# Three buffers freed in the output-weight stage, and expert weights laid out eight rows a partition

## The chip, the cores and the metric

The kernel runs on one NeuronCore of a Trainium2 chip. The metric is the device time of one execution in microseconds (us). Three runs of the kernel before took 727.13, 729.30 and 731.64 us; the median is 729.3. Lower is better.

## The reference, cut to what matters

Two transformer blocks over 256 tokens of width 1024, all float32. The first block has one layer: a hybrid mixer (three kinds of attention) and a hierarchical mixture of 32 experts. The second has two layers of attention.

```
y = hybrid_mixer(x, w_in, w_out, ...)            # heads A, B, C joined, then @ w_out (1024 x 1024)
x = layer_norm(ALPHA * x + y, ln1_g, ln1_b)
grp = argmax(x @ w_route_group + b)              # router: one of 4 groups,
top_val, top_idx = top_k(x @ w_route_expert, 2)  # then 2 of its 8 experts
y_e = (silu(x_e @ w_gate[e]) * (x_e @ w_up[e])) @ w_down[e]   # w_gate, w_up: 1024 x 256, w_down: 256 x 1024
x = layer_norm(ALPHA * x + sum of gate * y_e, ln2_g, ln2_b)
x = second_block(x, mem_2, ...)                  # two layers
```

The kernel reads the weights of all 32 experts, 1 MiB for each of gate, up and down (96 MiB).

## The kernel before, in words

**Engines.** The program is one instruction stream per engine. SP issues nearly all weight loads, in one fixed order; each may first wait on a semaphore, and every later load stands behind it. PE multiplies, ACT and DVE copy, normalise and split, POOL issues small loads and the vectors of the layer norms.

**Memory.** `ring` holds 12 slots of 1 MiB (8 KB in each of 128 partitions). Before the expert stage the same bytes have other names (the `with nc.sbuf_tensor` block): slots 0 to 4 receive raw weights, slots 5 to 7 are `w_high`, 8 to 10 `w_low`, 11 `a_high`. `x_low` shares its bytes with `xT`, `mix_low` with `mixT`. Nine more buffers of 1 MiB outside the ring also receive expert weights: halves of `bias`, `probsT`, `mixT`, `xT`, `k_c`, two parts of `tiles`, and the top of `values` (`beyond_ring`).

**Three products for one.** Before the experts, float32 accuracy comes from three products: weights and inputs are split into a high part (ACT, `high`, L1664) and a low part (DVE, `low`, L2336); `product` (L909 to L911) multiplies high by high, high by low and low by high. `SPLITS` lists the splits, `SPLIT_AT` the job at which each is made. `w_high` and `w_low` go round in six half-slot units. The jobs `tile1` and `bv` are input products; `y1` (s, tt) is one 256-column block s of the output product for token half tt. Their order is `Y_ORDER`, then come `x1t` (x turned), `logit` (router) and `rank`.

**Between y1 and the experts.** DVE takes each y1 into `x2` (L1959), forms mean and variance, then `centred` (L2110, two halves of 512) and `scaled` or `scaled_half` (L2118, L2124). The router works on x as it is ahead of the norm: PE turns it, ACT writes it to `xT` (L1504), PE multiplies (L1073). `choose`, `rank` and `locate_first` give every token its place in the experts' rows.

**The expert stage.** Experts are handled in 8 bunches of 4. Each bunch has 12 loads of 1 MiB: item j = 0 to 3 the first half of the 1024 input rows of gate and up for its four experts, j = 4 to 7 the second half, j = 8 to 11 the down weights. Below, expert load n is item n % 12 of bunch n // 12. PE's order in bunch b: `gate_up` half 0 and half 1 (L1324, 32 matmuls each), `gather` of bunch b + 1 (L1280: x is the stationary operand, 128 x 128 pieces), `turn_hidden` (L1299), `down` (L1339), `add_back` (L1307, into PSUM banks 0 to 3). In bunch 0, after gate_up half 1, four `diagonal` products put ALPHA * x in these banks (L1413). Between add_back of bunch 6 and gate_up of bunch 7 stands a test of a flag (`more_rounds`). In bunch 7 PE runs filling matmuls (L1271) ahead of down.

**Who frees a buffer.** `expert_slots` (L143 to L156) deals out buffers: loads 0 to 20 take those of `FIRST_LOADS`; four of them (`ONCE`) are used once; the other 17 go round in the order of the load's number. So load 21 takes load 0's buffer, and so on to load 83. For the last bunch the first four loads must take slots 0, 1, 2, 3 (`NEXT_LAYERS`), since the next layers' weights follow there. `free_for_experts` (L738) holds SP until the last user of that buffer is done, by `expert_done`: j < 4 after half 0 of gate_up, j < 8 after half 1 (`gu_ready`), j >= 8 after down (`y_ready`).

**The order of SP's work around the change** (`for n in range(FIRST_EXPERT)`, then `FIRST_LOADS`): w_out0, w_out1, w_out2 and w_out3 into slots 0, 1, 2, 0, w_out3 once w_out0 is split; load 2 into `k_c`; loads 16, 17, 18 once the last B scores are read; 3, 4 (`probsT`, top of `values`) once the attention is done; 5, 6, 7 into slots 1, 2, 0 once their weights are split; 8 to 15 as the y1 products release the split units; 19, 20. For bunches below `IN_ORDER` = 2 a partition holds rows p, p + 128, ... of gate and up (pieces of 1 KB); from bunch 2 on it holds eight adjacent rows (four to a half: 4 KB), and the gather takes x with a step of eight elements to match.

## Time and profile before

| | |
|---|---|
| median of 3 runs | 729.3 us |
| the profiled execution | 730.15 us |
| its span, first to last instruction | 728.2 us |
| mean granted TensorE clock | 0.969 |
| PE busy | 661.3 us (91%) |
| DVE, ACT busy | 353.1 us (48%), 330.1 us (45%) |
| moved by DMA | 167.84 MB, mean 230 GB/s |
| chain of waits by engine | PE 58%, SP's queue 13%, DMA 9%, DVE 8%, ACT 8%, issue 3% |

The page's busy shares are means over stages with different limits. It also cuts the span in 40 slices of 18.2 us; in its DMA line each digit is the busy share of the 16 DMA engines in tenths, and the line under it gives what they moved. Expert loads run from slice 4 on, the expert stage on PE from slice 10 to 22.

### The profile page before, as it was taken

To read this page: it belongs to the slowest core of one execution; us is meant where nothing else is said; L and a number is where in the kernel's file an instruction comes from. 1 tells how busy PE (TensorE), PEld (TensorE's weight loads), DVE (VectorE), ACT (ScalarE), POOL (GpSimd) and SP (SyncE) were. 2 spreads that over 40 slices of the span, in tenths; PEclk is the share of its full clock that TensorE was granted. 3 is DMA by queue.
4 is the path that set the end of the run, shared out by engine and by line. 5 is a ranking of instruction groups with operands and counts; after the bars stand their busy time and mean duration, and the time that the engine had idled before them with its cause. 6 is when DMAs were issued, how large, how long until landed. Compare 5 with 4: busy or idle time off the path is not lost.

```text
span 728.2 us, 11783 instructions
## 1 busy us (share of the span) xinstructions
PE 661.3 (91%) x4605; PEld 513.0 (70%) x4606; DVE 353.1 (48%) x817; ACT 330.1 (45%) x776; POOL 43.8 (6%) x57
## 2 busy tenths in 40 slices
PE   6989999999899999789796999898979999889986
PEld 5967998789545436335262589877859899778876
DVE  1543656645531021011010557787765487877733
ACT  3465656541011122011120354778864647788642
POOL 6001000000000000000000322000000020100000
PEclk9999999999999999898898999999979999999999
DMA  9995327097999999999999857045533080171301
GB/s 275 338 298 173 118 86 232 23 333 280 363 410 412 412 415 409 415 411 411 416 391 409 268 167 237 1 129 162 161 130 116 15 276 1 57 234 60 114 1 59
DMA packets 94682, 167.84 MB, mean 230 GB/s; under 512 B 4271, under 2 KB 75713, under 8 KB 90529
## 3 DMA queue, kind: packets, MB, share of 16 engines
q1 hardware_dynamic: 92272, 160.88, 61.5%
q0 software_dynamic: 2224, 6.10, 2.5%
q8 instruction: 39, 0.64, 0.4%
q14 instruction: 19, 0.15, 0.1%
q10 hardware_dynamic: 128, 0.08, 0.0%
HBM read 165.96 MB, written 1.07 MB: 229 GB/s over the span
## 4 chain that ended last, share of the span: by engine, by line
PE 58%; SPq 13%; DMA 9%; DVE 8%; ACT 8%; issue 3%; DVEq 0%; ACTq 0%
SPq L777 11%; PE psum L909 11%; PE psum L911 10%; PE psum L910 10%; PE psum L1324 4%; PE psum L1280 3%; DMA values<-in_w_expert_down_dram 3%; PE psum L1214 2%; DMA ring<-in_w_expert_up_dram 2%; PE psum L1339 2%; PE psum L952 2%; PE psum L1044 2%; PE psum L1261 2%; SPq L780 2%; DMA ring<-in_w_in_dram 2%
## 5 line engine op out<-in xcount | busy, mean ns | idle before, releaser
L909 PE MATMUL psum<-a_high,w_high 128*128 128x256 f32 x512 | 150.1, 293 | 8.7 <-DVE w_low L2336 4.6
L911 PE MATMUL psum<-a_high,w_low 128*128 128x256 f32 x512 | 145.4, 284 | 0.0
L910 PE MATMUL psum<-x_low,w_high 128*128 128x256 f32 x512 | 145.3, 284 | 0.0
L2336 DVE TENSOR_TENSOR w_low<-ring,w_high 128x1024 fp32r<-128x1024 f32 (+1 forms) x76 | 107.7, 1429 | 17.4 <-ACT w_high L1664 17.4
L909 PEld LDWEIGHTS psum<-a_high,w_high 128*128 128x128 f32 x512 | 98.6, 193 | 18.5 <-issue 6.8
L1664 ACT ACTIVATE w_high<-ring 128x1024 fp32r<-128x1024 f32 (+1 forms) x79 | 96.1, 1220 | 14.1 <-DMA ring<-in_w_in_dram 10.8
L910 PEld LDWEIGHTS psum<-x_low,w_high 128*128 128x128 f32 x512 | 98.7, 193 | 0.1
L911 PEld LDWEIGHTS psum<-a_high,w_low 128*128 128x128 f32 x512 | 98.6, 193 | 0.0
L1324 PE MATMUL psum<-ring,q_c 128*32 128x512 f32 x336 | 64.6, 708 | 13.5 <-DMA ring<-in_w_expert_up_dram 8.0
L909 PE MATMUL psum<-w_high,a_high 128*128 128x256 f32 x240 | 69.9, 291 | 0.1
L910 PE MATMUL psum<-w_low,a_high 128*128 128x256 f32 x240 | 68.7, 286 | 0.0
L1280 PEld LDWEIGHTS psum<-tiles,x_nat 128*128 128x128 f32 x256 | 53.6, 299 | 7.5 <-issue 7.5
L2258 DVE TENSOR_TENSOR tiles<-tiles,psum 128x256 f32<-128x256 f32 x8 | 3.4, 421 | 110.3 <-ACT tiles L1714 110.2
L1280 PE MATMUL psum<-tiles,x_nat 128*128 128x128 f32 x256 | 55.1, 373 | 0.5 <-DVE tiles L2231 0.5
L911 PE MATMUL psum<-w_high,mix_low 128*128 128x256 f32 x192 | 55.0, 286 | 0.0
L909 PEld LDWEIGHTS psum<-w_high,a_high 128*128 128x128 f32 x240 | 46.9, 195 | 3.6 <-issue 2.3
L1712 ACT ACTIVATE tiles<-psum 128x256 f32<-128x256 f32 x8 | 3.1, 384 | 99.9 <-PE psum L1324 99.9
L1324 PEld LDWEIGHTS psum<-ring,q_c 128*32 128x32 f32 x336 | 16.2, 127 | 44.0 <-issue 44.0
L910 PEld LDWEIGHTS psum<-w_low,a_high 128*128 128x128 f32 x240 | 47.0, 196 | 0.0
L911 PEld LDWEIGHTS psum<-w_high,mix_low 128*128 128x128 f32 x192 | 37.7, 197 | 0.0
L1214 PE MATMUL psum<-const,probs 128*128 128x128 f32 x200 | 32.6, 285 | 4.1 <-ACT probsT L1634 3.0
L1634 ACT ACTIVATE probsT<-psum 128x512 f32<-128x512 f32 (+1 forms) x56 | 30.3, 547 | 9.5 <-PE psum L1214 8.6
(343 smaller groups left out, 1148.1 us busy)
## 6 DMA issues: line engine op xcount, KB each, us to landing
ring<-in_w_in_dram SPq DMA_DIRECT2D x36, 1024.0 KB, 9.1
ring<-in_w_expert_down_dram SPq DMA_DIRECT2D x22, 1024.0 KB, 17.7
ring<-in_w_expert_gate_dram SPq DMA_DIRECT2D x42, 512.0 KB, 14.8
ring<-in_w_expert_up_dram SPq DMA_DIRECT2D x42, 512.0 KB, 15.3
ring<-in_w_out_dram SPq DMA_DIRECT2D x12, 1024.0 KB, 5.0
ring<-in_w_mem_kv_dram SPq DMA_DIRECT2D x4, 1024.0 KB, 12.2
k_c<-in_w_expert_down_dram SPq DMA_DIRECT2D x3, 1024.0 KB, 17.4
probsT<-in_w_expert_gate_dram SPq DMA_DIRECT2D x4, 512.0 KB, 15.0
```

The source lines that it names most:

```text
L777: sp.dma_start(to[:, SLOT // 2 * m:SLOT // 2 * m + SLOT // 2].rearrange("p (k n) -> p k n", n=DE), w[:, 4 * half:4 * half + 4, :]).then_in ...
L780: sp.dma_start(to, ins["w_expert_down"][0, e].rearrange("(p k) n -> p (k n)", p=P)).then_inc(loaded[slot_of(n)], 16)
L909: pe.matmul(dst, left[0], right[0], start=first, stop=False)
L910: pe.matmul(dst, left[0], right[1], start=False, stop=False)
L911: return pe.matmul(dst, left[1], right[0], start=False, stop=last)
L952: mm = pe.matmul(dst, src[:, k, P * tt:P * tt + P], w[:, k, a:b], start=(k == 0), stop=(k == KC - 1))
L1214: mm = pe.transpose(dst[:, P * c:P * c + P], pr[:, a:a + P], ident)
L1280: mm = pe.matmul(dst[:, P * c:P * c + P], x[:, k, :], places2[:, tt, :], start=(tt == 0), stop=(tt == 1))
L1324: mm = pe.matmul(bank(6)[PLACES * e:PLACES * e + PLACES, :], gathered2[b % 2][:, k, PLACES * e:PLACES * e + PLACES], w, start=(k == 0), st ...
L1634: act.activation(probsT[:, 512 * (n % 4):512 * (n % 4) + w], bank(t_at(n))[:, 0:w], ACT.Copy).then_inc(turned_out, 1)
L1664: act.activation(split_like_raw(n)[0], raw_of(n), ACT.Copy).then_inc(highs, 1)
L2336: dve.tensor_tensor(w_l, raw_of(n), as_f32(w_h), ALU.subtract).then_inc(lows, 1)
```

## The change

Six edits:

1. The low part of an output weight (`y1`) is written over its raw slot (`slots_low`, the same bytes as slots 0 to 4) and not into `w_low`. The slot is then free when the product has read it, not when it is split. w_out3 goes to slot 8 (`LAST_OUT_SLOT`) in place of slot 0.
2. The router's turned x goes to `q_c` (`x1T`), not to `xT`.
3. Slots 9 and 10 and `xT` take loads 4, 5 and 3 once the last input product (`LAST_INPUT`) is done. SP issues loads 2 and 3, then w_out3.
4. `FIRST_LOADS` has another order, and other buffers for loads 3 to 15 and 20.
5. `IN_ORDER` goes: gate and up weights lie eight rows a partition in all bunches.
6. The first norm writes x in the matching order: `centred` writes to `tiles`, `scaled_half` reads that and writes x with a step of 128 elements (`spread`). The gather then reads adjacent elements in all bunches; the diagonal products read with the step. Tokens 0 to 127 are scaled in two halves, not in one instruction.

```diff
@@ -130,15 +130,14 @@
 EARLY = ((0, 3), (1, 4))
-FIRST_LOADS = EARLY + ((2, K_C), (16, TILES_MID), (17, BIAS_HIGH), (18, BIAS_LOW), (3, PROBS_T), (4, V_TOP), (5, 1),
-                       (6, 2), (7, 0), (8, 6), (9, 9), (10, 7), (11, 10), (12, 5), (13, 8), (14, 11), (15, MIX_T),
-                       (19, LN_ROWS), (20, X_T))
+FIRST_LOADS = EARLY + ((2, K_C), (3, X_T), (4, 9), (5, 10), (16, TILES_MID), (17, BIAS_HIGH), (18, BIAS_LOW),
+                       (6, PROBS_T), (7, V_TOP), (8, 0), (9, 1), (10, 6), (11, 2), (12, 7), (13, 5), (14, 8), (15, 11),
+                       (20, MIX_T), (19, LN_ROWS))
 ONCE = (TILES_MID, BIAS_HIGH, BIAS_LOW, LN_ROWS)
...
 PER_BUNCH = 12
-IN_ORDER = 2
@@ -160,11 +159,14 @@
 TWICE_ROUND, LATE_RING = 2 * MIXERS_RING, 3
+LAST_OUT, LAST_OUT_SLOT = ITEM["w_out3"], 8
 MEM_AT = 3
...
 def slot_of(n):
+    if n == LAST_OUT:
+        return LAST_OUT_SLOT
     if n < FIRST_EXPERT:
@@ -386,7 +388,8 @@
-LAST_SPLIT = {item_split(n): n for n in range(len(SPLITS))}
+LAST_INPUT = max(n for n, _job in enumerate(JOBS) if _job[0] in ("tile1", "bv"))
+LAST_SPLIT = {item_split(n): n for n in range(len(SPLITS)) if SPLITS[n][0] != "y1"}
 OPENING = [SPLIT[("tile1", 0)]] + [SPLIT[("tile2", l, 0)] for l in range(LAYERS)]
@@ -436,7 +439,7 @@
-        with nc.sbuf_tensor("slots_before", [P, MIXERS_RING * SLOT], F32), \
+        with nc.sbuf_tensor("slots_low", [P, MIXERS_RING * SLOT], F32R) as slots_low, \
                 nc.sbuf_tensor("w_high", [P, UNITS * SLOT // 2], F32R) as w_high, \
@@ -469,6 +472,14 @@
+        def spread(row, half):
+
+            return row.rearrange("p (k q) -> p q k", k=KC)[:, P // 2 * half:P // 2 * half + P // 2, :]
+
+        def folded_in(row, half):
+
+            return row[:, 512 * half:512 * half + 512].rearrange("p (q k) -> p q k", k=KC)
+
         def c_(name):
@@ -477,7 +488,9 @@
         x4 = x_nat[:, :].rearrange("p (t k q) -> p t k q", t=2, k=KC)
+        centred2 = tiles[:, 0:2048].rearrange("p (t d) -> p t d", t=2)
         xT3 = xT[:, :].rearrange("p (k t) -> p k t", k=KC)
+        x1T = q_c[:, :].rearrange("p (k t) -> p k t", k=KC)
         y_nat = tiles[:, 0:2048].rearrange("p (t d) -> p t d", t=2)
@@ -487,7 +500,11 @@
             a = units_before(n) % UNITS * KC * P
-            return [w[:, a:a + KC * wide].rearrange("p (k n) -> p k n", k=KC) for w in (w_high, w_low)]
+            high, low = w_high[:, a:a + KC * wide], w_low[:, a:a + KC * wide]
+            if SPLITS[n][0] == "y1":
+                k = slot_of(item_split(n))
+                low = w_low[:, 0:SLOT] if k == LAST_OUT_SLOT else slots_low[:, SLOT * k:SLOT * k + SLOT]
+            return [w.rearrange("p (k n) -> p k n", k=KC) for w in (high, low)]
@@ -744,10 +761,12 @@
                     sp.wait_ge(*expert_done(earlier[-1]))
-                elif k < MIXERS_RING:
+                elif k < MIXERS_RING or k == LAST_OUT_SLOT:
                     used_up(max(m for m in range(FIRST_EXPERT) if slot_of(m) == k))
-                elif k < RING - 1:
-                    owners = {UNIT_OWNER[u] for u in range(units_before(OPENING[1])) if u % UNITS // 2 == (k - 5) % 3}
+                elif k in (9, 10, X_T):
+                    sp.wait_ge(p_ready, LAST_INPUT + 1)
+                elif k < 8:
+                    owners = {UNIT_OWNER[u] for u in range(units_before(OPENING[1])) if u % UNITS // 2 == k - 5}
                     sp.wait_ge(p_ready, max(max(users(n)) for n in owners) + 1)
@@ -759,8 +778,6 @@
                     sp.wait_ge(ln_done, 2)
-                elif k == X_T:
-                    sp.wait_ge(p_ready, JOB[("logit", 1)] + 1)
                 else:
@@ -773,7 +790,7 @@
                     for m, name in enumerate(("w_expert_gate", "w_expert_up")):
-                        w = ins[name][0, e].rearrange("(k p) n -> p k n" if b < IN_ORDER else "(p k) n -> p k n", p=P)
+                        w = ins[name][0, e].rearrange("(p k) n -> p k n", p=P)
                         sp.dma_start(to[:, SLOT // 2 * m:SLOT // 2 * m + SLOT // 2].rearrange("p (k n) -> p k n", n=DE),
@@ -783,7 +800,11 @@
             for n in range(FIRST_EXPERT):
-                if n >= MIXERS_RING:
+                if n == LAST_OUT:
+                    for i in range(2, 4):
+                        load_expert(FIRST_EXPERT + i)
+                    sp.wait_ge(p_ready, LAST_INPUT + 1)
+                elif n >= MIXERS_RING:
                     used_up(max(m for m in range(n) if slot_of(m) == slot_of(n)))
@@ -799,7 +820,7 @@
                     sp.dma_start(bias3[:, 0:A_HEADS, :], shifted_rows(0, A_HEADS)).then_inc(bias_in, 16)
-            for n in [i for i, _ in FIRST_LOADS[len(EARLY):]] + list(range(len(FIRST_LOADS), PER_BUNCH * (BUNCHES - 1))):
+            for n in [i for i, _ in FIRST_LOADS[len(EARLY) + 2:]] + list(range(len(FIRST_LOADS), PER_BUNCH * (BUNCHES - 1))):
                 load_expert(FIRST_EXPERT + n)
@@ -1070,7 +1091,7 @@
                             from_act(("x1t", tt, k // 4))
-                        mm = pe.matmul(dst[:, 0:GROUPS + EXPERTS], xT3[:, k, P * tt:P * tt + P], router[:, k, :],
+                        mm = pe.matmul(dst[:, 0:GROUPS + EXPERTS], x1T[:, k, P * tt:P * tt + P], router[:, k, :],
                                        start=(k == 0), stop=(k == KC - 1))
@@ -1276,8 +1297,7 @@
                     for tt in range(2):
-                        x = x4[:, tt] if b < IN_ORDER else x2[:, tt, :].rearrange("p (q k) -> p k q", k=KC)
-                        mm = pe.matmul(dst[:, P * c:P * c + P], x[:, k, :], places2[:, tt, :],
+                        mm = pe.matmul(dst[:, P * c:P * c + P], x4[:, tt, k, :], places2[:, tt, :],
                                        start=(tt == 0), stop=(tt == 1))
@@ -1411,7 +1431,7 @@
                             pe.matmul(bank(m), diagonal[:, P * (m // 2):P * (m // 2) + P],
-                                      x2[:, m // 2, 512 * (m % 2):512 * (m % 2) + 512],
+                                      spread(x2[:, m // 2, :], m % 2),
                                       start=True, stop=False, skip_group_check=True)
@@ -1501,7 +1521,7 @@
                     tt, half = job[1:]
-                    op = act.activation(xT3[:, 4 * half:4 * half + 4, P * tt:P * tt + P],
+                    op = act.activation(x1T[:, 4 * half:4 * half + 4, P * tt:P * tt + P],
                                         src.rearrange("p (c t) -> p c t", c=4), ACT.Copy)
@@ -2107,7 +2127,8 @@
                 for half in range(2):
-                    op = dve.scalar_tensor_tensor(x_half(tt, half), values(tt, half), mv3[:, tt, 0:1],
+                    to = x_half(tt, half) if n else centred2[:, tt, 512 * half:512 * half + 512]
+                    op = dve.scalar_tensor_tensor(to, values(tt, half), mv3[:, tt, 0:1],
                                                   ln_row[:, 0, 512 * half:512 * half + 512], ALU.subtract, ALU.mult)
@@ -2120,9 +2141,9 @@
-                xs = x_half(tt, half)
-                return dve.scalar_tensor_tensor(xs, xs, ln_rs[:, tt:tt + 1],
-                                                ln_row[:, 1, 512 * half:512 * half + 512], ALU.mult, ALU.add)
+                return dve.scalar_tensor_tensor(spread(x2[:, tt, :], half), folded_in(centred2[:, tt, :], half),
+                                                ln_rs[:, tt:tt + 1], folded_in(ln_row[:, 1, :], half),
+                                                ALU.mult, ALU.add)
@@ -2455,8 +2476,10 @@
                         centred(0, tt, ln1_in, x_half)
+                        dve.wait_ge(ln_rstd, tt + 1)
                         if tt == 0:
-                            scaled(0, 0)
+                            scaled_half(0, 0)
+                            scaled_half(0, 1).then_inc(ln_done, 1)
                         logit_shift(tt)
...
                             scaled_half(1, 0)
```

`spread(row, half)` is row viewed as 64 groups of 8 elements that lie 128 apart; `folded_in` views 512 adjacent elements as 64 groups of 8.

## Rows read from the trace of the kernel before

**Rows 1.** Chain that ended last, 343 to 404 us: start, us, what.

```profile
343.11 15.92 DMA ring<-in_w_expert_up_dram
...
359.17 6.62 PE psum L1324 x32
...
365.80 0.33 SPq L777
...
380.36 21.86 DMA values<-in_w_expert_down_dram
...
402.35 1.88 PE psum L1339 x13
```

**Rows 2.** The page's DMA share and rate in 40 slices.

```profile
DMA  9995327097999999999999857045533080171301
GB/s 275 338 298 173 118 86 232 23 333 280 363 410 412 412 415 409 415 411 411 416 391 409 268 167 237 1 129 162 161 130 116 15 276 1 57 234 60 114 1 59
```

**Rows 3.** Windows: bounds, length, busy per engine, clock, DMA share, GB/s.

```profile
129.00:143.00 14.00, 12.51 (x85) 9.71 (x84) 8.57 (x24) 7.30 (x16) 0.00 (x0) 1.00 0.00 1
...
186.00:198.00 12.00, 9.77 (x79) 6.40 (x77) 4.97 (x25) 1.06 (x3) 0.00 (x0) 1.00 1.10 350
205.00:359.00 154.00, 136.04 (x822) 72.40 (x820) 18.94 (x52) 25.80 (x55) 1.79 (x3) 0.95 1.02 412
```

**Rows 4.** SP's issues in order of time; below, landing of the downs issued near 173.

```profile
142.99 0.37 SPq L777 DMA_DIRECT2D tiles<-in_w_expert_gate_dram  x1
...
152.60 0.37 SPq L777 DMA_DIRECT2D probsT<-in_w_expert_gate_dram  x1
...
177.96 0.80 SPq L780 DMA_DIRECT2D ring<-in_w_expert_down_dram  x2
...
DMA to landing us min/median/max: 4.7/5.9/8.6
```

**Rows 5.** PE's timeline, end of the last input product.

```profile
131.26 0.28 PE L911 MATMUL psum<-w_high,x_low 128*128 128x256 f32 x1
```

**Rows 6.** DVE's timeline: y1 (1,1) and (2,1) taken from PSUM.

```profile
164.32 0.42 DVE L1959 SCALAR_TENSOR_TENSOR x_nat<-x_nat,psum 128x256 f32<-128x256 f32 x1 [0.26 <-PE psum L911]
...
172.96 0.42 DVE L1959 SCALAR_TENSOR_TENSOR x_nat<-x_nat,psum 128x256 f32<-128x256 f32 x1 [0.89 <-PE psum L911]
```

**Rows 7.** Chain, 188 to 220 us: bunch 0's gate_up half 0, diagonal, down.

```profile
192.08 3.64 PE psum L1324 x32
...
202.03 3.63 PE psum L1413 x8
...
210.19 3.69 PE psum L1339 x32
```

**Rows 8.** Groups of L1280: gather of bunch 1, twice, then bunch 2's weight loads.

```profile
L1280 PE MATMUL psum<-tiles,x_nat 128*128 128x128 f32 x32 | 3.7, 275 | 0.0
...
L1280 PEld LDWEIGHTS psum<-tiles,x_nat 128*128 128x128 f32 x31 | 3.5, 192 | 0.2 <-issue 0.2
...
L1280 PEld LDWEIGHTS psum<-tiles,x_nat 128*128 128x128 f32 x32 | 7.7, 334 | 0.8 <-issue 0.8
```

**Rows 9.** DVE's scaled_half: group from 170 to 192 us, and the last one.

```profile
L2124 DVE SCALAR_TENSOR_TENSOR x_nat<-x_nat,small,tiles 128x512 f32<-128x512 f32 x2 | 1.5, 751 | 0.1
...
187.75 0.75 DVE L2124 SCALAR_TENSOR_TENSOR x_nat<-x_nat,small,tiles 128x512 f32<-128x512 f32 x1
```

**Rows 10.** PE's timeline, bunches 6 and 7.

```profile
365.67 7.88 PE L1280 MATMUL psum<-tiles,x_nat 128*128 128x128 f32 x32
...
374.52 3.64 PE L1339 MATMUL psum<-ring,tiles 128*32 128x512 f32 x32 [0.51 <-ACT tiles L1719]
...
387.51 6.48 PE L1324 MATMUL psum<-ring,q_c 128*32 128x512 f32 x34 [4.78 <-issue]
...
396.93 1.99 PE L1271 MATMUL psum<-const 128*128 128x256 f32 x8
...
400.29 1.56 PE L1271 MATMUL psum<-const 128*128 128x256 f32 x6 [0.47 <-ACT tiles L1719]
```

## The prediction

> **What bounds the kernel now.** I read the chain of waits for the middle of the span first. Near the end of the expert stage it is one line [rows 1]: a load lands at 359.03 us, PE works 6.62 us, SP then issues the last bunch's loads from 365.80, and the last of these lands at 402.22, where PE begins the last down product. The page's DMA line [rows 2] shows nines from slice 9 to 21 and a 0 in slice 7. So weights bound the stage to about 402 us, and the DMA engines idle just before it. The windows give the rates [rows 3]: 1 GB/s from 129 to 143 us, 350 GB/s from 186 to 198 (bunch 1's gate and up weights in 1 KB pieces), 412 GB/s from 205 to 359 (4 and 8 KB pieces). A load of 1 MiB (1.049 MB) thus takes 3.0 or 2.545 us. After 402 us all follows that landing: next weights queue behind it, and the tail (728.2 - 402.35 = 325.9 us) is the same before and after.
>
> I number the 96 expert loads 0 to 95, twelve a bunch; 0 to 20 fill the 21 first buffers, 17 of which go round. Load 79 ends bunch 6's gate and up weights (landing 359.03), 80 to 83 are its down weights, 84 to 95 the last bunch.
>
> **The start of the stage.** Issue to landing on idle engines is 4.7 us for a down load [rows 4], so a restart costs 4.7 - 2.545, say 2.1 us, beyond the bytes. From code and rows, with the change:
> - the last input product ends at 131.5 [rows 5]. Loads 3, 4, 5 and w_out3 go out then: 131.5 + 2.1 + 3 x 2.545 + 3.0 = 144.2. These 3 MiB fill the idle stretch.
> - 16, 17, 18 wait for the last B scores (issue 142.99 [rows 4]): done 144.2 + 7.6 = 151.8.
> - 6, 7 (issue 152.60 [rows 4]): 154.7 + 5.1 = 159.8.
> - 8 needs w_out0 read to its end: two y1 jobs of 2.9 us before 164.3 [rows 6], 158.5; done 163.1. 9 needs w_out1: 164.3; done 168.9. 10, 11 wait for 173.0 [rows 6]: done 180.2.
> - 12 to 15 and 20 wait for the last y1 job (177.96 [rows 4]); they run 180.2 to 192.9, load 19 to 195.4.
>
> Now all buffers are full. Load 21 needs the first half of bunch 0's gate and up product, 192.08 + 3.64 = 195.7 [rows 7]; data flows again at 195.8 + 2.1 = 197.9. Before, load 20 landed at 359.03 less 61 MiB (loads 21 to 79, and 2 MiB from POOL's queue) x 2.545 = 203.8. So of 8.4 us (203.8 - 195.4) 2.5 are lost to full buffers, and **load 79 lands 5.9 us earlier, at 353.1**, if nothing else runs dry.
>
> Eight rows a partition (4 KB pieces in bunches 0 and 1) adds nothing: at 3.0 us a load the refill would end at 197.7, still ahead of 197.9. Its saving lies inside the wait for a buffer.
>
> **The small edits.** In-place low parts: the same DVE instruction count and shapes, no cost. x1T in q_c, the centred values in tiles: same instructions, other addresses, 0. scaled(0,0) in two halves: one more DVE instruction (2 x 0.75 for 1.28 us), in a stretch where DVE next waits for PE; hidden by that y1 job, +0.2 if the cover went. w_out3 comes at 139 us, is split near 158. SP stands at LAST_INPUT with load 3: behind it are w_out3 and loads that can't start sooner, none late for PE. No POOL instruction moves.
>
> Gather: from bunch 2 on its weight loads step 32 bytes and take 334 ns, with adjacent elements 192 [rows 8]; 32 pairs take 7.88 against 3.7 us [rows 8, 10]. Now all are adjacent: -4.15 us of PE work a bunch for six bunches. DMA bounds bunches 4 to 7, so it counts only where PE is on the chain, below.
>
> **The layout's price.** Two scaled_half instructions (0.75 us each, one seen at 187.75 [rows 9]) lie ahead of the first gather; they now write with a step of 512 bytes. Four logical diagonal matmuls (eight instructions, 3.63 us [rows 7]) read x with that step. No row shows either. Bounds: nothing; or the pace of the stepped weight load, 7.88/32 = 246 ns for 128 elements, 1.92 ns each. At this pace a 512-element DVE write takes 0.98 us (+0.24, twice 0.5) and a matmul 0.98 instead of 0.45, eight of them +4.2. I take the stepped price for both: that row is the nearest, and the lower end asks that a step cost nothing where it nearly doubled a weight load. A gain is excluded: no work is removed from these instructions.
>
> The Trainium skill (SBUF — State Buffer, "Door 1: The DMA port swizzle") says that SBUF lines hold 16 bytes and that each access to a new line pays. It speaks against this write and this read; the 32-byte row agrees, and no row here tests the rule on DVE. By it the term stands, without it the sum is 2.5 lower.
>
> Effect: +0.5 moves everything. The +4.2 delays bunch 0's down product from 213.9 [rows 7] to 218.6, and load 29 needs its buffer. Loads 21 to 28 keep the engines busy to 197.9 + 0.5 + 20.4 = 218.8; load 29 flows at 218.6 + 0.1 + 2.1 = 220.8: a **gap of 2.0 us**. Together **+2.5**.
>
> **The end of the stage: the wait that takes the gain.** The buffers go round in another order. Load 84 must be in slot 0. Before, slot 0 held load 79 last (7, 28, 45, 62, 79), so SP waited for gate_up(6): the issue at 365.80. Now slot 0 holds 8, 29, 46, 63, 80, a down weight, and 84 waits for **y_ready of bunch 6**; behind it on SP stand all twelve loads of the last bunch. With L for load 79's landing: gate_up(6) ends L + 6.75 (half 1 at the low clock). From there to the end of down(6) it was 378.16 - 365.78 = 12.38 us [rows 10]; less 4.15 for the gather, 8.23. SP issues at L + 15.1. Loads 80 to 83 are done at L + 10.2, so the engines stand dry for 7 us with the restart. Data ends at L + 15.1 + 2.1 + 12 x 2.545 = L + 47.7; before it was L + 43.2. **+4.5.**
>
> Then PE becomes late. The first half of gate_up(7) starts at load 87's landing, L + 27.4 (PE is ready at L + 24.4, with the 9.35 us from down(6) to 387.51 that stood before it [rows 10]), takes some 5.9 us as then (32 of the 34 matmuls in 6.48), and PE idles again until load 91, L + 37.6. If the clock is low again, as after the wait ahead of 359.17 [rows 1], half 1 takes 6.6 us, and 4.9 more pass to the end of the filling matmuls (396.93 to 401.85 [rows 10]): L + 49.1, against 402.35 before, L + 43.3. **+5.8** in place of 4.5; if the clock is up, 4.5.
>
> **Sum**: -5.9 + 0.5 + 2.0 + 5.8 = +2.4; I give +2.2 since the low clock of the last term isn't certain. The profiled execution took 730.15 (span 728.2 and 1.95 around it), 0.85 above the median of the three runs; I add the difference to the median: 729.3 + 2.2 = **731.5 us**.
>
> **Rivals.**
> - B, the gain stays. Slot 0 is free in time or the stop costs little, and the steps are cheap: -5.9 to -3.4, so 723.4 to 725.9; with the dry 2.5 us of the start gone as well, 721. For it: 3 MiB do fit in the idle stretch. Against it: the order of slots is fixed in the code, and [rows 1] show the last bunch's issue on the chain even before. Chance 0.17.
> - C, slower. Place: the eight diagonal matmuls in bunch 0. If each reads its operand twice at 1.92 ns an element, it takes 1.97 us, together +12.1: down(0) at 226.5, load 29 flows at 228.7, dry for 9.9 instead of 2.0. Sum +10.3, about 739.5. It decides from 0.7 us an instruction, where the gap opens (2.1 us of margin over eight). For it: the stepped weight load; against it: weight loads are read once here and matmuls may be too. Chance 0.08.
> - D, the early loads don't come early (LAST_INPUT satisfied late, w_out3 in their way). The refill ends 7.6 us later, 203.0, and is not dry: -0.8 at load 79, so -0.8 + 0.5 + 5.8 = +5.5 (the gap at load 29 goes, since the queue is fuller): 734.8. Chance 0.07.
> - A, my forecast with its bounds: without step costs and with the clock up, -5.9 + 4.5 = -1.4 (727.9); with gather(6) at the low clock, 3.7 more (735.2). Chance 0.68.
>
> **Numbers.** A change under 1% (7.3 us) cannot be told from none. A and D lie within it, B nearly all (I leave 0.10 for below 722.0), C and a wider A above 736.6, 0.10. So faster 0.10, same 0.80, slower 0.10. A alone reaches 727.9 to 735.2; the range goes down into B to 723.4 and up to 736.2, leaving out the ends of B and C.
>
> **What would show it.** Right: DMA idle from 132 to 143 gone; a dip near 195 to 198; load 79 about 5 us earlier; SP's first issue of the last bunch after the end of down(6), not after gate_up(6), with DMA near 0 for some 7 us before it; gather 3.7 us throughout; diagonal matmuls near 1 us. Wrong: no dip ahead of the last bunch (B), or L1413's successor at 0.6 us (then -2.0), or at 2 us (C). It would also fail if DMA's rate fell where loads and products meet in new ways.

## The result, and the profile after

The changed kernel takes **736.23 us** (median of nine executions, 734.07 to 738.01) against 729.3 for the kernel before on the same chip: a ratio of 1.010, 95% interval 1.0076 to 1.0133. It is 6.9 us slower. The prediction was 731.5, range 723.4 to 736.2, with 0.10 on slower by over 1%.

Medians here are of all executions; ratios leave out the few slow ones. The profiled execution took 736.33 us (span 734.2), 6.2 above that of before. On its page, the clock, the DMA share and the rate in 40 slices, as in [rows 2]:

```profile
PEclk9999999999999999898895999999999999999999
DMA  9995325785999999999959928108173071082301
GB/s 273 340 291 178 118 79 173 260 304 215 357 393 361 411 416 409 414 413 413 415 196 416 365 89 289 53 25 263 58 229 111 5 250 39 2 268 76 115 1 58
```

Slice 7, 23 GB/s before, now moves 260: the idle stretch is filled. Slice 20, 391 before, is at 196: a new dry stretch near 375 us. SP's issues, as in [rows 4]:

```profile
131.88 0.33 SPq L794 DMA_DIRECT2D xT<-in_w_expert_gate_dram  x1
...
143.50 0.33 SPq L794 DMA_DIRECT2D tiles<-in_w_expert_gate_dram  x1
...
154.54 0.33 SPq L794 DMA_DIRECT2D probsT<-in_w_expert_gate_dram  x1
...
198.24 0.80 SPq L797 DMA_DIRECT2D ring<-in_w_expert_down_dram  x2
```

The early loads leave at 131.88 and all 21 buffers are full before 198.24, when load 21 may go. Bunch 0 on the chain, as in [rows 7]:

```profile
194.55 3.64 PE psum L1344 x32
...
204.50 7.09 PE psum L1433 x8
...
216.12 3.69 PE psum L1359 x32
```

and the groups of the gather's weight loads, the diagonal products and the split scaling, as in [rows 8] and [rows 9]:

```profile
L1300 PEld LDWEIGHTS psum<-tiles,x_nat 128*128 128x128 f32 x64 | 7.5, 192 | 2.8 <-issue 2.8
...
L1433 PE MATMUL psum<-x_nat,diagonal 128*128 128x512 f32 x8 | 7.2, 1049 | 0.0
...
L2144 DVE SCALAR_TENSOR_TENSOR x_nat<-tiles,small 128x512 f32<-128x512 f32 x1 | 1.1, 1112 | 0.0
```

The eight diagonal products take 7.09 us instead of 3.63, a stepped DVE write 1.11 instead of 0.75, and the gather's weight loads 192 ns. The chain of the last two bunches, as in [rows 1]:

```profile
345.18 15.91 DMA values<-in_w_expert_up_dram
...
361.23 5.34 PE psum L1344 x32
366.56 3.78 PE psum L1300 x32
...
371.29 3.69 PE psum L1359 x32
374.99 0.33 SPq L794
...
385.34 15.26 DMA mixT<-in_w_expert_up_dram
...
400.73 6.15 PE psum L1344 x32
...
410.13 1.56 PE psum L1292 x6
411.69 1.41 PE psum L1359 x9
```

Load 79 lands at 361.09, 2.1 us later than before and not 3.4 earlier. SP then issues the last bunch only after down(6), the down product of bunch 6 (L1359 at 371.29): it does so at 374.99, and the last down product begins at 411.69, 9.3 us later than before. Windows around the new stop (bounds, length, busy per engine, clock, DMA share, GB/s):

```profile
370.00:374.00 4.00, 3.50 (x35) 1.51 (x38) 0.42 (x1) 1.47 (x3) 0.00 (x0) 1.00 0.00 2
374.00:376.00 2.00, 1.68 (x17) 0.64 (x10) 0.69 (x1) 0.44 (x2) 0.00 (x0) 1.00 0.06 10
376.00:378.00 2.00, 2.00 (x5) 0.87 (x5) 0.00 (x0) 1.13 (x4) 0.00 (x0) 1.00 0.82 233
378.00:380.00 2.00, 1.51 (x4) 0.38 (x2) 0.00 (x0) 0.00 (x0) 0.00 (x0) 1.00 0.97 231
380.00:384.00 4.00, 0.00 (x0) 0.00 (x0) 0.00 (x0) 0.00 (x0) 0.00 (x0) 0.73 1.01 386
```

The DMA engines are dry (they move next to nothing) to 376, and then, though they are 82 to 97% busy, they move 231 to 233 GB/s for 4 us. That was in no term of the prediction.

### The profile page after: what moved, and what is told of

It reads as the page before. It is cut to its first block, busy times and chain, and to the rows that moved or that the text cites. A ratio compares the mean times of both kernels' runs of the same rounds, so it can differ in the third digit from the quotient of the medians.

```text
span 734.2 us, 11785 instructions
## 1 busy us (share of the span) xinstructions
PE 639.6 (87%) x4605; PEld 489.0 (67%) x4606; DVE 353.9 (48%) x818; ACT 330.0 (45%) x776; POOL 43.7 (6%) x57
## 4 chain that ended last, share of the span: by engine, by line
PE 58%; SPq 14%; DVE 10%; ACT 7%; DMA 7%; issue 3%; DVEq 0%; ACTq 0%
SPq L794 12%; PE psum L930 10%; PE psum L931 9%; PE psum L932 9%; PE psum L1344 4%; PE psum L973 4%; DMA ring<-in_w_in_dram 3%; PE psum L1235 2%; DMA values<-in_w_expert_up_dram 2%; DMA mixT<-in_w_expert_up_dram 2%; PE psum L1300 2%; PE psum L1359 2%; PE psum L1065 2%; PE psum L1282 2%; SPq L797 2%
## 5 line engine op out<-in xcount | busy, mean ns | idle before, releaser
L2357 DVE TENSOR_TENSOR w_low<-ring,w_high 128x1024 fp32r<-128x1024 f32 (+1 forms) x73 | 100.9, 1395 | 17.9 <-ACT w_high L1684 17.9
L931 PE MATMUL psum<-w_low,a_high 128*128 128x256 f32 x192 | 54.3, 283 | 0.0
L931 PEld LDWEIGHTS psum<-w_low,a_high 128*128 128x128 f32 x192 | 36.8, 192 | 0.0
L1300 PEld LDWEIGHTS psum<-tiles,x_nat 128*128 128x128 f32 x256 | 29.4, 192 | 7.8 <-issue 7.8
L1327 PE MATMUL psum<-values,tiles 128*128 128x512 f32 x64 | 29.4, 602 | 4.9 <-DVE values L2285 4.9
## 6 DMA issues: line engine op xcount, KB each, us to landing
ring<-in_w_mem_kv_dram SPq DMA_DIRECT2D x4, 1024.0 KB, 15.1
```

Of the source, the lines that this page charges most:

```text
L931: pe.matmul(dst, left[0], right[1], start=False, stop=False)
L1300: mm = pe.matmul(dst[:, P * c:P * c + P], x4[:, tt, k, :], places2[:, tt, :], start=(tt == 0), stop=(tt == 1))
L1327: mm = pe.matmul(bank(2 * tt + half), back[:, P * tt:P * tt + P], y_e[:, 512 * half:512 * half + 512], start=False, stop=last, skip_group_ ...
L2357: dve.tensor_tensor(w_l, raw_of(n), as_f32(w_h), ALU.subtract).then_inc(lows, 1)
```

## The experiments

Each was timed in five rounds beside the kernel before. L is the landing of load 79, I the issue of load 84, D the start of the last down product, all from the one profiled execution (L of e1, e11, e16 and e17 is the start of the product that waits for the load, less the 0.14 us that lie between the two in the other rows). Each ratio is known to 0.3 or 0.4%, so a difference between two of these kernels is known to 3 or 4 us: e1's 7.3 is clear of that, differences near 3 us are not, and for them L, I and D say where the time went in one execution.

| kernel | median us | ratio (95%) | L | I | D |
|---|---|---|---|---|---|
| before | 729.3 | 1 | 359.03 | 365.80 | 402.35 |
| changed | 736.23 | 1.0104 (1.0076 to 1.0133) | 361.09 | 374.99 | 411.69 |
| e1 | 728.96 | 0.9999 (0.9969 to 1.0029) | 364.09 | 356.41 | 406.27 |
| e2 | 733.09 | 1.0064 (1.0031 to 1.0098) | 358.22 | 371.93 | 408.35 |
| e3 | 736.24 | 1.0103 (1.0067 to 1.0138) | 359.14 | 373.51 | 410.43 |
| e4 | 730.27 | 1.0009 (0.9976 to 1.0042) | 360.13 | 366.25 | 402.28 |
| e5 | 735.21 | 1.0094 (1.0055 to 1.0133) | 358.06 | 375.90 | 411.65 |
| e6 | 724.67 | 0.9929 (0.9897 to 0.9961) | 358.75 | 350.99 | 401.41 |
| e7 | 740.15 | 1.0129 (1.0076 to 1.0181) | 360.86 | 375.22 | 411.99 |
| e9 | 737.05 | 1.0108 (1.0063 to 1.0153) | 359.75 | 374.80 | 410.76 |
| e10 | 732.70 | 1.0045 (1.0010 to 1.0080) | 359.16 | 373.93 | 408.23 |
| e11 | 728.98 | 0.9995 (0.9959 to 1.0030) | 358.74 | 350.97 | 400.15 |
| e13 | 736.32 | 1.0078 (1.0043 to 1.0113) | 360.97 | 374.88 | 408.75 |
| e16 | 725.84 | 0.9937 (0.9895 to 0.9978) | 357.94 | 350.15 | 399.28 |
| e17 | 723.18 | 0.9908 (0.9871 to 0.9946) | 354.99 | 347.27 | 396.65 |
| e18 | 732.75 | 1.0049 (1.0020 to 1.0079) | 355.70 | 370.26 | 404.54 |

**e1, other slots for the last bunch.** In the assignment of buffers, bunch 6's down weights may not take the next layer's slots, one of which load 84 needs:

```
+        downs = i >= PER_BUNCH * (BUNCHES - 2) and j >= 2 * AT_ONCE
-        at.append(next(k for k in free if not last or ...
+        at.append(next(k for k in free if (k not in NEXT_LAYERS or not downs) and (not last or ...
```

> The changed kernel, only that bunch 6's four down weights may not take slots 0 to 3. Slots 0 to 2 then last held gate and up weights of bunch 5, and the last bunch's first loads wait for nothing late. Theory W (the new wait for down of bunch 6 is the largest loss): SP issues load 84 right behind load 83, the dry stretch of 5.4 us (370.5 to 376.0) and the slow restart behind it go, last load lands some 43 us after load 79 and not 49.7, time 6 to 8 us less than the changed kernel's 736.2: 728 to 730. Rival (the loss lies at the start, and the end would be bound by PE anyway): 0 to 2 us less, 734 to 736.

Measured: 728.96, 7.3 us less, and SP no longer waits for down(6). Its chain:

```profile
356.41 0.33 SPq L795
...
383.69 22.45 DMA ring<-in_w_expert_down_dram
...
406.27 3.67 PE psum L1360 x32
```

One slot's order is the whole loss against before. What is then missing is the gain. (D is late in this profile because the stage began late in it, at 197.70 against 194.55, with the clock at 0.66 from 140 to 150 us.)

**e2, diagonal products that read x adjacent** (in the changed kernel).

```
-  spread(x2[:, m // 2, :], m % 2),
+  x2[:, m // 2, 512 * (m % 2):512 * (m % 2) + 512],
```

> The changed kernel, only that the four diagonal products read 512 adjacent elements of x, so the sums get other features than they should; work and shapes are the same. Theory S (the step of 512 bytes makes a matmul read slow): eight instructions go from 7.1 back to 3.6 us, down of bunch 0 ends 3.5 us earlier, and load 29 is not late; total 2 to 4 us less, 732 to 734. Rival (the bubble is filled later anyway, since DMA bounds the stage): PE's 3.5 us go, total within 1 us of 736.2.

Measured: 733.09, 3.1 less, at the edge of what the intervals can tell; the eight take 3.6 us again, and with the same start (194.64) load 79 lands 2.87 us earlier (358.22).

**e3, DVE's scaling written adjacent.** `spread(x2[:, tt, :], half)` and its two inputs become plain halves.

> The changed kernel, only that DVE scales x with adjacent reads and writes, so x lies in natural order where the gather expects the other; work and shapes are the same. Theory S for DVE: 1.11 us a half go back to 0.75, of the two or three on the path 0.7 to 1.1 us come off; total 0.5 to 1.5 us less, 735. Rival (the 2 us by which bunch 0 began late are DVE's steps): 2.5 us less.

Measured: 736.24, so the stepped DVE write costs nothing that the median can tell. Its stage began at 193.30, e18's, which has the step and the same clock in every 10 us from 100 to 200, at 193.54: 0.24 us.

**e4, the layout edits alone on the kernel before.**

> The kernel before with the layout edits alone: eight rows a partition in all bunches, x normalised into interleaved columns in two halves, diagonal products with a stepped read. Buffers and their order are those of before. Theory: the sum of the terms that the changed kernel's trace shows without the buffers. DVE +0.4 to 0.7 us and the eight diagonal instructions near 7.1 us instead of 3.63, which matters only if bunch 0's down product is late for load 29; gather 3.7 us from the third bunch on instead of 7.88, of little use while weights bound the stage; the 1 MiB loads of bunches 0 and 1 at 412 instead of 350 GB/s once the engines are warm, but every load of them that starts on idle engines runs at 210 to 260 GB/s for some 4 us. SP issues the last bunch after gate_up(6), so no dry stretch ahead of it. Together 727 to 732 us, most likely 730. Rival (the layout alone is what made the changed kernel slow): over 733.

Measured: 730.27, as the theory had it. Without the early loads and the new order of slots the layout's steps are hidden.

**e5, the buffer edits alone** (layout of before: `IN_ORDER = 2`, x in plain order, stepped gather).

> The changed kernel without the layout: three buffers freed early, the new order of loads and slots, but 1 KB pieces in bunches 0 and 1, gather with a step of eight elements from bunch 2 on, x in natural order. By W the wait for down of bunch 6 stands, and the 7.9 us gather now lies ahead of it, so load 84 goes out 18 us after load 79 lands (13.9 in the changed kernel); against that no stepped reads or writes, and restarts with 1 KB pieces. Sum from 729.3: 5 to 6 earlier at load 79, then 9 to 10 later: 732 to 735. Rival (layout is the whole loss, buffers bring what they free): 722 to 726.

Measured: 735.21. The chain and one window:

```profile
342.08 15.98 DMA values<-in_w_expert_up_dram
...
363.43 7.83 PE psum L1302 x32
...
372.20 3.69 PE psum L1361 x32
...
375.90 0.33 SPq L795
```

```profile
368.00:376.00 8.00, 7.49 (x52) 4.67 (x52) 0.52 (x2) 1.53 (x4) 0.00 (x0) 1.00 0.00 1
```

The DMA engines stand for 8 us, since a gather of 7.83 us, and not of 3.78, lies on the path to SP's issue.

**e6, the buffer edits alone with e1's rule.**

> The buffer edits alone (low parts in place, x elsewhere, early loads; layout of before), and the last bunch's first gate and up weights in slots that bunch 6's down weights don't hold. Theory (the wait for bunch 6's down product took the gain): the run with the buffers alone stood dry for 8.3 us ahead of the last bunch and took 735.2; without the dry stretch 7 to 8 us less, and 2 to 3 more from down(6) no longer being on the chain, but PE, with the 7.88 us gather, may then be late: 724 to 728, best estimate 726.5, below the changed kernel with that rule alone (728.96). Rival (the 3 MiB gained in the idle stretch are worth nothing since the stage is bound by PE by then, or by the weights' later rate): 729 or more, with PE busy without a gap from 390 us.

Measured: 724.67, faster than before by 0.7%, and 10.5 us less than e5 (12 by the ratios). PE is late at the end, as the rival had it, without the rival's time:

```profile
387.22 9.38 PE psum L1347 x64
...
399.85 1.56 PE psum L1294 x6
401.41 3.62 PE psum L1362 x32
```

**e7, up weights from the other half's rows.** `w[:, 4 * (half ^ m):4 * (half ^ m) + 4, :]`.

> The changed kernel, where each up weight's half load takes the rows of the other half (the products use rows that don't belong to them; everything else is as in the changed kernel, the same bytes and instructions). Theory R, that the gate and up pieces of a half load lie at the same offset in every 8 KB and so fall on the same part of the memory when queues are short: with half of the pieces from the other offset the restarts after the two dry stretches run faster, at 350 GB/s or more in the windows right after 375 us where the changed kernel shows 213 to 254, and the total is 2 to 4 us less, 732 to 734. Rival (the slow restart comes with the number of requests outstanding, whatever their addresses): 213 to 260 GB/s again, and 736 us.

Measured: 740.15, a miss for both. The windows from 376 us show 188, 385 and then 353 GB/s, about as many bytes over the first 8 us as in the changed kernel. Gate and up are separate requests, so every request still read at one offset; the idea of a shared offset was left standing for a wider test. The extra 4 us lie behind the stage: its last down product starts at 411.99, 0.3 us after the changed kernel's, and from there to the end it takes 326.2 us against 322.5, with the clock low in three places (see 7 below).

**e9, 1 KB pieces in bunches 0 and 1.** `rearrange("(k p) n -> p k n" if b < 2 else "(p k) n -> p k n")`.

> The changed kernel, with the gate and up weights of bunches 0 and 1 read in 1 KB pieces as before (x keeps its new layout, so their products mix rows that don't belong together; bytes and instructions are as in the changed kernel). My prediction gave the eight rows a partition nothing in bunches 0 and 1: 736 within 1 us, with the slower 350 GB/s hidden by the wait for a buffer. Theory R: 1 KB pieces start at once at 380 GB/s after each stop, so the early loads come no later and the resume near 200 to 212 us is faster by about 1 us, against 0.45 us a load lost in warm stretches: 735 to 738. Rival (the pieces' rate bounds the refill): 3 to 5 us slower, 739 or more.

Measured: 737.05 (six executions). Eight rows a partition in the first two bunches add nothing that can be told, as predicted.

**e10, four adjacent rows a partition.** A half load becomes one block of 512 rows, with x interleaved by four:

```
-  w = ins[name][0, e].rearrange("(p k) n -> p k n", p=P)
+  w = ins[name][0, e].rearrange("(h p k) n -> h p k n", h=2, k=4)
...
-  w[:, 4 * half:4 * half + 4, :]).then_inc(loaded[slot_of(n)], 16)
+  w[half]).then_inc(loaded[slot_of(n)], 16)
```

> The changed kernel with another layout of the gate and up weights: a half load takes 512 adjacent rows, four to a partition, so its pieces are still 4 KB but lie back to back instead of at every second 4 KB; x is interleaved to match. Everything else, steps of the reads and writes included, is the same. Theory R in its wider form (the pieces at a pitch of 8 KB all begin in the same part of the memory): the restart after the dry stretch near 376 us runs at 350 GB/s or more at once instead of 232 over the first 4 us, likewise near 200 to 212 and 224 us, and the kernel takes 732 to 734. Rival (4 KB pieces start slowly wherever they lie): 210 to 290 GB/s again over 4 us, and 736 us.

Measured: 732.70, 3.5 less, again at the edge of the intervals. The issue is at 373.93, 1.06 us earlier than in the changed kernel; the same windows as above:

```profile
374.00:376.00 2.00, 1.68 (x7) 0.90 (x7) 0.63 (x1) 1.50 (x4) 0.00 (x0) 1.00 0.54 135
376.00:378.00 2.00, 2.00 (x6) 0.76 (x4) 0.00 (x0) 0.07 (x1) 0.00 (x0) 1.00 1.00 401
378.00:380.00 2.00, 0.45 (x2) 0.00 (x0) 0.00 (x0) 0.00 (x0) 0.00 (x0) 1.00 1.00 391
```

Counted from the issue, the second microsecond moves 213 GB/s in the changed kernel and 221 here. The next three move 254, 221 and 242 GB/s there, at a pitch of 8 KB (pieces that begin 8 KB apart), and 410, 401 and 377 here, with the same 4 KB back to back. It repeats: 217 to 270 GB/s in e2, e3, e5 and e9, which have the pitch, 381 to 422 in e18, which doesn't. From load 84's issue to load 91's landing it is 23.99 us instead of 25.61, and to the last down product 34.30 instead of 36.70. Of these 2.4 us only 1.6 are the loads'; 0.8 come from the second half of gate_up(7), which ran at a higher clock (5.37 us and not 6.15).

**e13, 8 KB pieces in the last bunch** (its gate and up loads read rows of the down weights).

> The changed kernel, where the eight gate and up loads of the last bunch read rows of the down weights, in 8 KB pieces and one request each (their products are of other weights; the same bytes and the same instructions on the compute engines). If the size of the piece, or its pitch, makes the slow restart, the first 4 us after the dry stretch run at 380 GB/s or more, load 84 to 95 land 1.5 to 2 us sooner and the kernel takes 734 to 735. Rival (every load after a dry stretch of this length starts slowly): 232 GB/s as in the changed kernel, 736 us.

Measured: the stage is faster; that the kernel is, the runs don't show. 283 and then 410 GB/s, between the two forecasts at first, where the changed kernel has 233 and 231:

```profile
376.00:378.00 2.00, 2.00 (x6) 0.81 (x5) 0.00 (x0) 1.01 (x3) 0.00 (x0) 1.00 0.77 283
378.00:380.00 2.00, 1.40 (x4) 0.33 (x2) 0.00 (x0) 0.00 (x0) 0.00 (x0) 1.00 0.98 410
```

The last down product starts at 408.75, 2.9 us earlier, and yet the median is that of the changed kernel. The ratio is 1.9 us lower, inside the intervals. In the profile the time comes back behind D, 325.9 us against 322.5.

**e16, e1 and e2 together.**

> The changed kernel with two of its costs taken away together: the last bunch's first loads in slots that bunch 6's down weights don't hold, and the diagonal products reading x adjacent (they then copy columns in another order). If the wait and the stepped read are two separate costs, they add up: 736.2 - 7.3 - 3.1 = 725.8, so 724.5 to 727.5, as good as the kernel with the buffer edits alone and the other slots (724.7). Rival (with the wait gone the start is hidden, so the stepped read costs nothing): 728 to 729.

Measured: 725.84. By the ratios the sum is 0.9959 (1.0104 less 0.0105 and 0.0040), and 0.9937 (0.9895 to 0.9978) was measured: wait and stepped read add up, as separate costs do. That the medians agree to 0.1 us is luck.

**e11, e1 and e10 together.**

> The changed kernel with other slots for the last bunch and four adjacent rows a partition in each half load; it computes the reference in full. With the wait gone 728.96 was measured; if the pitch of the pieces makes the slow starts, 1.5 to 3 us less, 726 to 727.5; if not, 729.

Measured: 728.98, as e1: a miss. With the wait gone the pitch costs the whole kernel nothing that can be told. In the stage it may still cost: e11's load 79 lands 5.35 us ahead of e1's, of which its earlier start (194.51 against 197.70) is 3.2; but behind D e11 takes 3.6 us more (324.7 against 321.1).

**e18, e10 and e2 together.**

> The changed kernel with four adjacent rows a partition in each half load and the diagonal products reading x adjacent (they then copy columns in another order), so that of its costs only the wait for bunch 6's down product is left. If the slow restarts (3.5 measured) and the stepped read (3.1 measured) are separate costs: 736.2 - 3.5 - 3.1 = 729.6, so 728.5 to 731. Rival (they overlap, since both are paid in bunch 0): 731.5 to 733.

Measured: 732.75, the rival's number, but the trace shows the theory's stage:

```profile
339.74 15.96 DMA values<-in_w_expert_up_dram
...
370.26 0.33 SPq L794
...
404.54 3.62 PE psum L1359 x32
```

Against the changed kernel the last down product is 7.15 us earlier; e10 and e2 alone gave 3.46 and 3.34. In the stage the costs add up. 3.5 us come back behind it (326.0 against 322.5), where this execution's clock was low:

```profile
530.00:545.00 15.00, 11.10 (x67) 7.03 (x66) 10.43 (x23) 9.23 (x25) 0.00 (x0) 0.77 0.51 172
```

**e17, the best version.** e6 with e10's adjacent rows from the third bunch on; x stays in plain order, and the gather steps by 16 bytes:

```
+  x = x4[:, tt, k, :] if b < IN_ORDER else \
+      x2[:, tt, 512 * (k // 4):512 * (k // 4) + 512].rearrange("p (q k) -> p k q", k=4)[:, k % 4, :]
```

> The kernel with the buffer edits alone and the other slots (724.67), its weights from the third bunch on read as four adjacent rows a partition in each half load; the gather then steps over x in 16 bytes instead of 32. It computes the reference in full. If a step of 16 bytes costs the weight load as much as one of 32, the gather stays at 7.8 us; if less, between 3.7 and 7.8. With weights in time to the last bunch neither the pitch nor the gather is on the path for more than 1 us: 723 to 725. Rival (adjacent pieces are slower in the warm stretch): 726 or more.

Measured: 723.18, ratio 0.9908 (0.9871 to 0.9946), 13 us below the changed kernel and 6.8 below the kernel before timed beside it (729.98); that it beats e6 (1.5 us) is within the intervals. The profile is of its fastest execution (719.58). Its chain, and the group of the gather from the third bunch on:

```profile
375.42 21.10 DMA ring<-in_w_expert_down_dram
...
396.65 3.67 PE psum L1362 x32
```

```profile
L1303 PEld LDWEIGHTS psum<-tiles,x_nat 128*128 128x128 f32 x46 | 10.9, 329 | 0.8 <-issue 0.8
```

## Why the prediction was wrong, and where it was right

Its mechanism held: the early loads come, the buffers fill, and the new order of slots makes the last bunch wait for down(6), which takes the gain and more (e1: 7.3 us). **What failed are two terms of the sum**, 3.4 us gained at load 79 and 5.8 us lost behind it; by the profiled executions load 79 came 2.1 us later and 7.3 were lost behind it. The step behind both that the experiments show is the price of a restart, 2.1 us, which was 5.2 for the last bunch (4 below).

1. **The start**, given +0.5, was +2.5 (194.55 against 192.08). The clock stood at 0.83 from 140 to 150 us, where before it was 1.00:

```profile
140.00:150.00 10.00, 9.13 (x45) 6.40 (x46) 5.00 (x14) 5.10 (x12) 0.00 (x0) 0.83 1.00 340
```

 It stood at 0.83 again from 180 to 190 (such a figure is a mean of the full clock, 1.00 or 2.4 GHz, and the low one, 0.50 or 1.2 GHz). The same two stretches and a start of 194.63 stand in e4's profile, which has no early loads, and e17's profile, which has them, shows 1.00 throughout and 192.23. The other twelve have at least one stretch of 10 us at 0.66 or 0.83 between 140 and 200 us and start at 193.30 to 197.70. So the start goes with the clock of the execution. What sets the clock was not found; whether the change makes low stretches likelier is open too, since the kernel before has one profile.

2. **The early loads**, -5.9. In e18, which has neither the stepped read nor the pitch, load 79 lands 3.3 us earlier than before (355.70 against 359.03) with a start 1.5 late (193.54): -4.8 of the -5.9. e17 gives it with before's start (192.23) and 1 KB pieces in bunches 0 and 1: -4.0 (354.99). The term was 1 to 2 us too large.

3. **The stepped read**, priced 4.2 for the eight and 2.0 for its gap at load 29. The eight rose by 3.5; e2 gained 2.9 at load 79 and 3.1 in all. So the price per instruction was a little high and its effect a little low. The DVE steps, priced at 0.5, cost 0.36 us an instruction (1.11 against 0.75) and 0.24 at the start (e3 against e18). Rival C (two reads of the operand) is out: 1.05 us an instruction, not 1.97.

4. **The restart**, taken at 2.1 us beyond bytes that flow at 412 GB/s, is the term that was mis-sized. [Rows 4] showed it for 8 KB down pieces on idle engines, and I used it for 4 KB gate and up pieces at a pitch of 8 KB, which before never started on idle engines. They run at 231 to 233 GB/s for 4 us. From load 84's issue to load 91's landing the changed kernel took 25.6 us; the bytes are 8 x 2.545 = 20.4, so the restart was 5.2 us and not 2.1. e10 gives the pitch's share: 1.9 us at load 79 (359.16 against 361.09, same start) and 1.6 here. With adjacent pieces the restart is still 3.6 us, with 8 KB pieces (e13, 23.56 us) 3.2; what these hold beyond 2.1 no run shows. e10's 34.30 us from issue to down product lie near the prediction's 34.0 (L + 49.1 less L + 15.1) by luck: its restart was 1.5 us longer and its half of gate_up(7) 1.2 shorter. The Trainium skill (DMA: Bandwidth & Descriptors, "Latency and other measured facts") tells of copies that ran at 103 GB/s with rows 4 or 8 MiB apart and at 214 with the 4 MiB padded by 4 KiB, and infers that partitions in lockstep fall on the same memory channels. The runs here show a like loss at 8 KB, but only after a stop; that channels are the cause no run shows.

5. **SP's issue**, predicted L + 15.1, came at L + 13.9, since the clock rose in time for gate_up(6) (5.34 us and not 6.6). This took 1.2 us off the second term.

6. **The sizes together.** At load 79 the error is 5.5 us: 2.0 start, 1.9 pitch, 0.9 stepped read (2.9 against 2.0), and 0.7 that lies within the shortfall of the early loads (2 above). Behind it 1.5: 3.1 for the restart, less 1.2 for SP's issue and 0.4 for the half of gate_up(7), which took 6.15 us and not 6.6.

7. **"The tail is the same"** failed by the other sign. Behind D the profile of before had 325.9 us (728.2 - 402.35), that of the changed kernel 322.5. The like stretches, before and then after, 132 to 150 us behind D:

```profile
534.35:552.35 18.00, 15.18 (x92) 12.54 (x93) 8.78 (x16) 9.62 (x19) 0.00 (x0) 0.72 0.14 43
```

```profile
543.69:561.69 18.00, 13.26 (x105) 11.63 (x106) 10.08 (x19) 10.99 (x24) 0.00 (x0) 1.00 0.26 79
```

 With 9.3 at D and -3.3 behind it the spans' difference of 6.0 is told in full. This was luck for the number: with the tail of before the changed kernel's profile would have been 3.3 us longer. Span less D is 321.0 to 322.6 us in the profiles of e1, e2, e5, e6, e9, e10 and e17, and 324.7 to 327.3 in those of e3, e4, e7, e11, e13, e16 and e18. So the tail differs by 3 us and more between executions of kernels that have the same instructions there; where it is long, windows of low clock like the one of before stand in it. Taken in stretches of 10 us from D, the clock is 1.00 in all of them in e1, e9 and e17 (tail 321.0 to 321.1); one is at 0.83 in the changed kernel, e2, e5, e6 and e10 (322.4 to 322.6); three or more are at 0.67 to 0.85 in before and the seven others. Whether that explains e13's and e18's missing 3 us in the median too isn't shown, since only profiled executions show their stages. But these two profiled executions (736.56 and 732.55) lie within 0.3 us of their medians, as do those of the changed kernel, e2 and e10.

Right: no dry stretch from 132 to 143; the gather at 3.8 us; nothing from eight rows a partition (e9); the last bunch's issue behind down(6); and PE late at the last half, idle twice for weights. The range missed the time by 0.03 us; its upper end had no restart slower than 2.1 us in it, and 0.10 for slower by over 1% was too little for a change whose gain had to pass through one new wait.

## What to carry to other kernels

When a ring of buffers is permuted, list for the first load of each later stage which product frees its slot: here one line in that assignment is worth 7.3 us, more than all that the freed buffers brought. Price a restart by the kind of load that restarts, not by the nearest load on idle engines, and where loads may restart after a stop, lay half loads out so that their pieces are adjacent in memory. A gain of a few microseconds in one stage is of the size that the clock takes or gives in another, so read it at the stage's end as well as in the total.

## What the runs showed of the hardware

- Gate and up pieces of 4 KB at a pitch of 8 KB run at 231 to 233 GB/s for 4 us after a stop, while the engines are 82 to 97% busy; adjacent ones reach 401 to 410 a microsecond after they begin (e10). In the warm stretch the pitch costs nothing (412 GB/s [rows 3]).
- An fp32 operand read with a step of 512 bytes takes a diagonal product from 605 to 1049 ns, not to twice that.
- A step of 16 bytes costs a weight load 329 ns, one of 32 bytes 334 [rows 8], adjacent elements 192. By the line of 16 bytes that the Trainium skill gives (SBUF — State Buffer, "Door 1: The DMA port swizzle") every element of either step opens a new line, and the rows agree.
- The last 320 us took 321.0 to 321.1 us at a granted clock of 1.00 throughout, 322.4 to 322.6 with one stretch of 10 us at 0.83, and 324.7 to 327.3 with three or more low ones.
